# Products of the identity with itself on TensorE: in the routing chain, ahead of the first gather of the expert stage, and at the end of the joining stage

## The reference, cut to what matters

```python
probs = softmax(t @ w_router);  sel = probs + b_router
gsel = argmax(top_k(sel.reshape(-1, 4, 4), 2)[0].sum(-1))
_, eidx = top_k(where(in_grp, sel, -inf), 2)
act = silu(gu[..., :256]) * gu[..., 256:] * gates
y = einsum('tef,efd->td', act, w_down)
```

## Time and profile before

| | |
|---|---|
| median of three runs | 2130.65 us (2125.85 to 2142.84) |
| the profiled execution | 2116.55 us, span 2114.7 us |
| mean granted TensorE clock of the profiled execution | 0.928 |
| PE busy (matmuls) | 1819.8 us, 86% of the span |
| DVE, ACT, POOL busy | 793.4, 379.9, 358.8 us |
| moved by DMA | 399.62 MB, mean 189 GB/s |

### The profile page before, as it was taken

How to read it: one execution, slowest core, us unless ns; L and a number is a source line. 1 busy time by engine, 2 the same in 40 slices (tenths; PEclk the granted TensorE clock), 3 DMA queues, 4 the chain that set the end, 5 groups by cost and what they waited for, 6 DMA issues and landing times. The chain is left out here.

```text
span 2114.7 us, 37006 instructions
## 1 busy us (share of the span) xinstructions
PE 1819.8 (86%) x15669; PEld 965.3 (46%) x15669; DVE 793.4 (38%) x1655; ACT 379.9 (18%) x839; POOL 358.8 (17%) x461
## 2 busy tenths in 40 slices
PE   6999999999999778956989989988988889949980
PEld 4344444444444432324556665765754454433320
DVE  0233332323423410024765565556544443340006
ACT  1010000000000011214332242232233120001212
POOL 0020110201103110022531122031022001220106
PEclk9999999999999789977999989999999899959985
DMA  9546666365551399968422034033134467178973
GB/s 325 192 165 237 245 211 243 142 229 199 181 189 60 108 391 401 397 258 268 134 82 63 11 114 127 12 106 111 28 126 135 162 199 238 43 284 310 401 294 137
DMA packets 236590, 399.62 MB, mean 189 GB/s; under 512 B 17977, under 2 KB 91953, under 8 KB 236370
## 3 DMA queue, kind: packets, MB, share of 16 engines
q1 hardware_dynamic: 230474, 375.75, 50.9%
q0 software_dynamic: 5952, 21.50, 2.7%
HBM read 303.71 MB, written 93.51 MB: 188 GB/s over the span
## 5 line engine op out<-in xcount | busy, mean ns | idle before, releaser
L682 PE MATMUL bank<-ring,hT 128*128 128x512 f32 x704 | 319.5, 601 | 1.9 <-DVE ret_qk L900 1.9
L1353 PE MATMUL bank<-hT,ring 128*128 128x272 f32 x768 | 216.4, 416 | 0.0
L682 PEld LDWEIGHTS bank<-ring,hT 128*128 128x128 f32 x704 | 129.6, 191 | 170.0 <-issue 169.8
L2530 PE MATMUL bank<-expert_w,exp_xT 128*32 128x512 f32 x1152 | 181.0, 637 | 14.2 <-DMA expert_w<-in_moe_w_gu_dram 10.3
L1353 PEld LDWEIGHTS bank<-hT,ring 128*128 128x128 f32 x768 | 140.5, 196 | 33.5 <-issue 8.7
L1347 PE MATMUL bank<-ring,hT 128*128 128x512 f32 x256 | 122.3, 606 | 0.0
L3343 PE MATMUL bank<-ring,oT 128*128 128x512 f32 x248 | 112.7, 614 | 0.8 <-PEq L576 0.8
L2530 PEld LDWEIGHTS bank<-expert_w,exp_xT 128*32 128x32 f32 x1152 | 48.0, 116 | 128.1 <-issue 122.9
L2554 PE MATMUL bank<-expert_w,exp_aT 128*32 128x512 f32 x576 | 90.6, 621 | 16.9 <-DMA expert_w<-in_moe_w_down_dram 15.5
L2626 DVE TENSOR_TENSOR exp_a<-bank,exp_sg 128x256 f32<-128x256 f32 x24 | 10.2, 425 | 221.1 <-ACT exp_sg L2608 221.1
L974 DVE SCALAR_TENSOR_TENSOR ret_Ss<-ret_Ss,ret_sdec,bank 128x512 f32<-128x512 f32 x64 | 45.0, 745 | 121.3 <-PE bank L768 121.3
(11 more groups left out here) (529 smaller groups left out, 2714.2 us busy)
## 6 DMA issues: line engine op xcount, KB each, us to landing
expert_w<-in_moe_w_gu_dram SPq DMA_DIRECT2D x24, 2048.0 KB, 15.0
ring<-in_w_ada_dram SPq DMA_DIRECT2D x20, 2048.0 KB, 9.7
expert_outputs<-ret_zeros SPq DMA_DIRECT2D x15, 2048.0 KB, 10.2
expert_w<-in_moe_w_down_dram SPq DMA_DIRECT2D x24, 1024.0 KB, 16.4
ret_Ss<-in_state_ret_dram SPq DMA_DIRECT2D x32, 512.0 KB, 5.2
out_dram<-ret_Ss SPq DMA_DIRECT2D x32, 512.0 KB, 3.3
oT<-in_moe_w_gu_dram SPq DMA_DIRECT2D x8, 2048.0 KB
ring<-in_dn_w_in_dram SPq DMA_DIRECT2D x8, 2048.0 KB, 9.2
```

The lines of the kernel that those rows point to most:

```text
L682: last = pe.matmul(ps[u % 2][:, :], core.hT[:, k, tok(t)], core.ring[:, core.slot[w], k, :], start=(k == 0), stop=(k == KD - 1))
L1353: mm = pe.matmul(ps[U % 2][:, 0:HALF], core.ring[:, core.slot[w], k, c * P:(c + 1) * P], core.hT[:, k, half * HALF:(half + 1) * HALF], sta ...
L2530: last = pe.matmul(ps[v][G * j:G * (j + 1), :], xT[:, v, k, G * j:G * (j + 1)], wgu[of[j] % SLOTS][:, k, :], start=(k == 0), stop=(k == KD ...
```

## The change

A helper issues one product of the identity with itself, n times 128 columns wide. It is called in four places:

- in the routing chain, ahead of the wait for `both_done`: 15 products of 256 columns, each behind a wait for one more pair of DVE's steps (2, 4, ... 30);
- in the routing chain of layer 1 alone, after the ranks and ahead of the first wait for `lanes_done`: 6 products of 256 columns, behind steps 45, 47, ... 55;
- after the last product of the routing, ahead of the first `turn`: 8 products of 512 columns, with no wait;
- at the end of PE's program in the joining stage, after the last tile is turned: 5 products of 512 columns, with no wait.

```diff
+def idle_product(pe, core, bank, n):
+    pe.matmul(bank[:, 0:n * P], core.ident[:, :], core.ident[:, :].unsqueeze(1).broadcast_to([P, n, P]), start=True, stop=True)
 
     def ranks_and_lanes(pe):
+        for n in range(2, 32, 2):
+            pe.wait_ge(steps, n)
+            idle_product(pe, core, ps[3], 2)
         pe.wait_ge(both_done, 1)
...
+        if l:
+            for n in range(45, 57, 2):
+                pe.wait_ge(steps, n)
+                idle_product(pe, core, ps[3], 2)
         for j in range(2):
             pe.wait_ge(lanes_done, j + 1)
...
         last.then_inc(source_ps, 1)
+        for n in range(8):
+            idle_product(pe, core, ps[3], 4)
...
                         last.then_inc(s["cols_turned"], 1)
+                for n in range(5):
+                    idle_product(pe, core, ps[5], 4)
```

## The result

The changed kernel took **2134.43 us**, the median of 20 runs (2125.55 to 2141.8), against 2127.11 (2121.63 to 2142.84) for the kernel before in as many: ratio 1.003, interval 1.0016 to 1.0045. The forecast was 1.5 us less than before; measured are 7.3 more. Over all 45 runs its mean is 2133.1, that of all 169 runs of the kernel before (e1's included) 2128.2, so plus 4.9 us (standard error 1.0).

What follows compares the result with a forecast made beforehand. It saw PE at half clock delaying routing and gather, DMA bounding layer 0's experts, PE the delta net. Profiled 2116.55 us, minus 4.2 (layer 1), plus 2.7 (joining stage), gave 2115.0; on the median 2129.1, range 2121 to 2143.

Steps and rivals of the forecast that it cites:

- Net plus 2.7 us: Joining stage: five products start the delta net 4.9 us late and its warm start gives back 2.2.
- Between 0 and 1.5 us of waiting; I take 0: Delta net: PE's wait at the convolution's rows (L1368), whose loads are issued 4.9 us later.
- The burst: End of the joining stage: the five products end at 980.5, so the next stage starts 4.9 us late.
- The give-back of 2.2 us: Delta net: its cold start, 4.44 us at half clock, takes 2.2 at full clock.
- slower rival: Uncovered bursts: joining stage plus 4.9 with nothing given back, late ranks plus 5; plus 8 in all, 2138.7 us; chance 0.12.
- its ends, 979.4 and 981.3: Joining stage: when the five products end if transposes count towards the clock's rise, or if it rises late.
- minus 4.2 us: Layer 1's routing and gather: earlier `source`, warm transposes and first `up` shorten idle DMA; bounds minus 5.1 and 0.
- the clock falls anyway: Rival: clock falls before the first `turn`, leaving layer 1 minus 1.9; sum plus 0.8, 2131.5 us; chance 0.2.
- nothing: Layer 0's expert stage: the same edits gain nothing, hidden in the wait for weights; at most minus 3.8 without that cover.
- hidden: Rival: layer 1's gain is made up while DMA is full later; plus 2.7 in all, 2133.4 us; chance 0.1.
- every case would stay within 1%: Whole kernel: all cases lie within 1% (21 us) of the time before; chance of same 0.96.

Runs made afterwards that it cites:

- e1: The kernel before, unedited, profiled and timed once more against the kernel before: ratio 1.0006 (0.9985 to 1.0027).
- e2: Only the five products at the end of the joining stage added to the kernel before: ratio 1.0034 (1.0013 to 1.0055).
- e8: e2 with GpSimd's first delta net product held until VectorE has finished the gate rows: ratio to the kernel before 1.0008 (0.9989 to 1.0026).
- e10: The whole change with GpSimd's first delta net product held until VectorE has finished the gate rows: ratio to the kernel before 1.0024 (1.0002 to 1.0045).
- e4: e2 plus two 512-column products in the delta net just ahead of PE's wait for the convolution's rows: ratio to the kernel before 1.0017 (1.0001 to 1.0032).
- e5: The kernel before with the five products behind the barrier, first on PE in the delta net: ratio 1.0038 (1.0021 to 1.0056).
- e12: The whole change measured again against the kernel before: ratio 1.0003 (0.9979 to 1.0027).
- e13: The whole change measured again against the kernel before: ratio 1.0009 (0.998 to 1.0038).
- e14: The whole change measured again, a single run: 2139.94 us.
- e11: The routing and gather products in layer 1 alone, none in layer 0 or the joining stage, against the kernel before: ratio 0.9994 (0.9979 to 1.0009).
- e15: e11 timed once more, against the kernel before: ratio 0.9967 (0.994 to 0.9994).
- e3: The change without the joining stage's five products, against the kernel before: ratio 0.9999 (0.9977 to 1.0021).
- e17: Fifteen 128-column products in one burst at the start of layer 0's expert stage, added to the kernel before: ratio 0.998 (0.9954 to 1.0007).

## Why the prediction was wrong, and where it was right

**The sign was wrong, and the step that failed is the joining stage's "Net plus 2.7 us", with the line under it, "Between 0 and 1.5 us of waiting; I take 0".** The burst itself was sized well: 4.9 us late was forecast, and the stage is 4.9 us longer in the two profiles. The give-back of 2.2 us is what isn't there: PE had none of it left at the gate columns, 12.19 us into the stage's work instead of 11.75. PE arrived at the convolution's rows 0.84 us (e2: 1.39) before they had landed, and the clock fell for 3.4 us or more within the next few us. That fall, 7.3 to 8.6 us into the delta net, is in every profile of a kernel with the five products ahead of the barrier and nothing over the wait (the change four times, e2, e8, e10), and in none of the others. That the wait is what brings the fall is e4's part, in one profile: with products in front of it the clock stayed up there.

M says what is left: 126.1 to 127.1 in the three profiles of the change that don't collide, against a mean of 121.9 in the nine profiles without the products. That is plus 4.2 to 5.2 instead of plus 2.7. It rests on the mean: the nine lie 3.4 us apart, and against before's own 123.4, the highest of them, it would be 2.8 to 3.7. The timed runs can't tell the two sizes apart, as e8's interval (up to 1.0026) holds both. This is the slower rival's mechanism, nothing given back, at its plus 4.9. Its condition, a wait of over 2 us at those rows, was set too high: 0.84 was enough.

The prediction's own bounds for this term were also off. With 2.2 us given back its ends, 979.4 and 981.3, make plus 1.6 and 3.5, not 2.1 and 4.1, and the rise after 5 us that it chose makes plus 3.0, not the 2.7 of a rise after 4.4.

**What the prediction didn't have at all** is the meeting of GpSimd's rows and VectorE's gate rows. It asked what TensorE would do at the barrier, not what the later gate rows would meet. It is worth some 10 us in e5's profile. In e2's and in one of the change's four (e12) M is 8.5 and 5.7 us higher than in the profiles that don't collide (e8; e13 and e14), of which the longer fall ahead of the gate rows is 1.6 to 1.8; in the others the collision costs nothing. It probably explains the difference between e2 and e8 (1.0034 and 1.0008); for the whole change it isn't shown to matter much, as e10 isn't clearly faster.

**Layer 1, "minus 4.2 us", held.** `source` 1.4 us early (1.3 forecast), transposes and first `up` as forecast, 5.2 us early at its end (5.1 forecast), minus 3.6 in the measured mean of e11 and e15. The ranks were 0.3 us late (0.4 forecast). The stage's means (196.9 against 201.2) say minus 4.3. The mechanism was the stated one: the gap in which DMA stood idle. One step came out otherwise without harm: the clock fell during the eight products, which ended 0.69 us ahead of the first `turn` and not 2.5, and it was back by then. In all eight profiles with both parts the first `up` took 7.07 or 7.08 us, so "the clock falls anyway" did not happen in layer 1.

**Layer 0, "nothing",** has no clear answer. In the first profile its first `up` is warm and 3.1 us earlier, and the wait for weights takes it back, as forecast. The stage is 1.5 us longer in the profile, but 203.7 to 205.1 us in the other kernels, with or without products there.

**The sum.** With plus 4.2 to 5.2 in the joining stage and minus 4.2 in layer 1 the change should cost 0 to 1 us; with 5.7 us of collision in one execution of four, 1.4 to 2.4. All its runs say plus 4.9, standard error 1.0. e2 and e3 add up to it: their means are plus 6.5 (error 1.4) and minus 1.0 (1.9). What is missing, some 2.5 to 3.5 us, lies between e3 and e11 (minus 1.0 against minus 3.6), thus in layer 0's parts or behind them, and is within twice the errors of those means. One place is left open by M, which ends 77 us into the delta net: that whole stage took 783.7 to 791.4 us in all five profiles with every part of the change (e10 among them), 773.9 to 780.6 with the joining stage's products alone (e2, e4, e8), and 769.9 to 787.9 without them. No run separates that from chance, and the sum isn't settled. The rival "hidden" (plus 2.7 in all) is nearer by its size, but its mechanism, layer 1's gain made up later, is contradicted by e11 and e15. That every case would stay within 1% was right.

## What to carry to other kernels

Keeping TensorE's clock up paid here where the engine stood idle anyway and the work behind it bounded the next transfer (layer 1's gather and routing, 3.6 us). The burst in front of a barrier was paid in full, and what it saved was lost as soon as a load behind the barrier wasn't ready earlier too. Moving one engine by 5 us can push another's short instructions onto GpSimd's long ones: read by what margin they miss each other before.

## What the hardware did that I had not expected

- VectorE instructions of 0.24 us took 2.32 to 2.39 us beside a GpSimd instruction of 2.35 us, and ended with it; three of 128x568 that take 2.50 us together took 4.46 in e12 and 6.44 in e5.
- TensorE at full clock and busy 6.76 of 7.60 us still lost its clock after a wait of 0.84 us; e4, with 1.9 us of products in front of the same wait, kept it there.
- A stage with nothing changed in it became 2.8 us longer in the profile when fifteen products were added ahead of it in the program, 1030 us earlier in time (e17), without a measurable effect on the whole time.
- The delta net, 770.7 us in before's profile and 781.6 in that of the same kernel again, differs between them by more than the whole change is worth.
